# Runs of four U and four V rows instead of eight in the PEER gathers, and another place for the ranking

## The chip, the cores and the metric

The kernel runs on one core of a Trainium2 chip. The metric is the time of one execution in microseconds, measured on the device. Three runs of the kernel before gave 5031.24, 5041.35 and 5054.40 us; the median is 5041.35.

## The reference, cut to what matters

One inference step of a two-layer decoder: 512 prompt tokens and 64 sample tokens (8 sequences of 8), width 1024. Layer 0 mixes tokens with latent attention (the samples against 4096 cached positions each), layer 1 with sliding-window attention. After each of the two stands a PEER channel mixer, which is where this change lies:

```python
q = (xt @ w_q).reshape(n, PEER_HEADS, 2, PEER_HALF)
s = jnp.einsum('nhpd,hpkd->nhpk', q, sub_keys)
s_top, i_top = lax.top_k(s, PEER_TOPK)                 # 16 of 128, twice per head
cand_s = s_top[:, :, 0, :, None] + s_top[:, :, 1, None, :]
best_s, best_pos = lax.top_k(cand_s.reshape(n, 8, 256), PEER_TOPK)
experts = jnp.take_along_axis(cand_i, best_pos, axis=-1)
gates = jax.nn.softmax(best_s, axis=-1)
act = gelu(jnp.einsum('td,thkd->thk', x, u_tab[experts]))
out = jnp.einsum('thk,thkd->td', gates * act, v_tab[experts])
```

Eight heads choose 16 experts each, so every token reads 128 rows of `u_tab` and 128 of `v_tab`, each of 1024 float32 values (4 KB).

## The kernel before, in words

**Tiles and slots.** Tokens lie on the 128 partitions. There are four tiles of prompt tokens and one of the 64 sample tokens, which is put twice on the partitions, so that it needs half as many slots. A *slot* is one expert position for all 128 tokens of a tile: one gather of U (512 KB, 128 rows of 4 KB) and one of V. A layer has `ALL` = 4 x 128 + 64 = 576 slots, so 1152 gathers. The whole is done twice, by `peer_rows` for layer 0 and for layer 1.

**What a slot needs.** POOL issues both gathers as indirect DMAs (`gather`, L1550 to L1554). DVE multiplies the U row with the normed token and sums it (`dot`, L1582 to L1586). When all dots of a group of `RG` slots are there, ACT takes their gelu (`gelu`, L1773) and DVE multiplies by the gates (`coefs`, L1588). ACT makes a diagonal matrix of each slot's coefficient (`diagonal`, L1778) and PE multiplies it with the V row into two PSUM banks (`mix`, L1871). At the end of a tile DVE adds the banks to the residual (`add`, L1643).

**The ring.** Row buffers form a ring of 16 (`RING`). POOL gathers in runs: U of group 0, U of group 1, V of group 0, U of group 2, V of group 1 and so on, with 8 slots a group (L1561 to L1574). `u_th` and `v_th` (L1440, L1441) give a slot's place in that order. Gather n waits until gather n-16 has been used: for U by its dot (`S_uf`), for V by its mix (`S_vf`). POOL is in order, so one unfree buffer holds up all that come after.

**The order on the engines.** Each engine walks through `now` = 0 to 588 in an order written out by hand. At `now` DVE does `dot(now)`; at `now` = 1 modulo `RG` it does `coefs` of the group before; at 11 of a tile `add` of the tile before. ACT does `diagonal(now - 10)`, then, at a multiple of `RG`, `gelu` of the group that has just ended; PE does `mix(now - 12)`.

**Work for the next tile.** In between, DVE finds the experts of the next tile (L1746 to L1756): `rank` (the best 16 of 256 candidates of a head, eight operations) at 16, 24 to 72; `key_numbers` (three operations on 128 x 2048 elements for either half) at 80 and 84; `number` at 88; `gate` at 96. ACT takes `exps` at 92. POOL waits for `number` (`S_ex`) when it starts on a new tile.

**The first of the two layers** also carries the latent attention of the samples (`latent_step`, 4 steps for each of 72 parts, 16 steps to every 21 slots) and then the sample tile's own projections, keys and ranking (`sample_step`). Each latent step goes over PE, ACT and DVE in turn: DVE waits there for PE's scores (L1663), and ACT takes an exp (L1802), for which it has to load another table than for the gelu. In the second layer `latent` is None, so none of this is there.

Of the kernel before, what the change touches and what calls it, by code (L numbers as in the profile page):

```python
# [46 lines left out]
PH, NK, TOPK, HALF = 8, 128, 16, 128  # L47
# [1196 lines left out]
def rank_head(nc, ch, settled, halves, ranks, hd):  # L1244


    def ranked(ins):
        ch.inc(ins)
        wait_apart(ch.eng, ch.done, ch.base + ch.n, settled)
    cand, rest, best, place = ranks["cand"], ranks["rest"], ranks["best"], ranks["place"]  # L1250
    flat = cand[:].rearrange("p i j -> p (i j)")
    ranked(nc.vector.tensor_tensor(cand[:], halves[0].unsqueeze(2).to_broadcast([P, TOPK, TOPK]),
                                   halves[1].unsqueeze(1).to_broadcast([P, TOPK, TOPK]), ALU.add))
    ranked(nc.vector.max(best[:, 0:8], flat))
    ranked(nc.vector.max_index(place[:, 0:8], best[:, 0:8], flat))
    ranked(nc.vector.match_replace(rest[:], best[:, 0:8], flat, -3e38))
    ranked(nc.vector.max(best[:, 8:16], rest[:]))
    ranked(nc.vector.max_index(place[:, 8:16], best[:, 8:16], rest[:]))
    ch.inc(nc.vector.tensor_copy(ranks["all_best"][:, bass.ds(hd * TOPK, TOPK)], best[:]))
    ch.inc(nc.vector.tensor_copy(ranks["all_places"][:, bass.ds(hd * TOPK, TOPK)], place[:]))  # L1260
    wait_apart(ch.eng, ch.done, ch.base + ch.n, settled)
# [150 lines left out]
def peer_rows(nc, a, sbuf, sem, bank, x, ident, mod, junk, stat, layer, h2, best, key, ranks, mod_rows, landed, latent=None):  # L1412
# [1 line left out]

    tag = f"px{layer}_"
    s = ExitStack()
    RG = 8
    RD = 8
    KEEP = 4 * RG
    ALL = NTP * HK + PAIRED  # L1420
    GROUPS = ALL // RG
    PER_TILE = HK // RG
    DIAG_AT, MIX_AT = 10, 12
    ST = NTP * HK - HK
# [14 lines left out]
    bvt, bpt = ranks["all_best"], ranks["all_places"]  # L1439
    u_th = lambda slot: slot if slot < RG else slot // RG * 2 * RG - RG + slot % RG  # L1440
    v_th = lambda slot: (slot // RG + 1) * 2 * RG + slot % RG if slot < ALL - RG else slot + ALL  # L1441
    landings = lambda n: 16 * (layer * (2 * ALL // RING) + n // RING + 1)
# [10 lines left out]
    if latent is not None:  # L1453
# [46 lines left out]
        def latent_steps(now):  # L1500
            return range(-(-16 * now // 21), min(-(-16 * (now + 1) // 21), 4 * (PARTS + 1)))
# [5 lines left out]
    with nc.Block() as block:  # L1507
# [40 lines left out]
        @block.gpsimd  # L1548
        def _(pool):
            def gather(table, slot, n):  # L1550
                if n >= RING:
                    freed, slots = released(n - RING)
                    pool.wait_ge(freed, slots)
                pool.indirect_dma_start(row_buf[n % RING][:], None, table, offset(ap=experts[:, slot:slot + 1], axis=0)).then_inc(landed[n % RING], 16)  # L1554

            def released(n):
                return (S_uf, u_slot[n] + 1) if n in u_slot else (S_vf, v_slot[n] + 1)

            u_slot = {u_th(slot): slot for slot in range(ALL)}
            v_slot = {v_th(slot): slot for slot in range(ALL)}  # L1560
            for g in range(GROUPS + 1):  # L1561
                if g < GROUPS:
                    if g % PER_TILE == 0:
                        pool.wait_ge(S_ex, g // PER_TILE + 1)
                    if latent is not None and g == 53:
                        pool.wait_ge(S_xss, 1)
                        nc.gpsimd.tensor_tensor(sq[:, 1:2], sq[:, 0:1], stat[:, 3:4], ALU.add).then_inc(S_add, 1)
                        pool.wait_ge(S_add, 1)
                        nc.gpsimd.tensor_tensor(sq[:, 1:2], sq[:, 1:2], stat[:, 4:5], ALU.pow).then_inc(S_xr, 1)
                    for slot in range(g * RG, (g + 1) * RG):  # L1570
                        gather(u_tab, slot, u_th(slot))
                if g >= 1:
                    for slot in range((g - 1) * RG, g * RG):
                        gather(v_tab, slot, v_th(slot))  # L1574

        @block.vector
        def _(dve):
# [4 lines left out]
            def dot(slot):  # L1582
                dve.wait_ge(landed[u_th(slot) % RING], landings(u_th(slot)))
                u = row_buf[u_th(slot) % RING]
                nc.vector.scalar_tensor_tensor(out=u[:], in0=u[:], scalar=1.0, in1=h2[:, tile_of(slot), :], op0=ALU.mult, op1=ALU.mult,  # L1585
                                               accum_out=dots[:, slot % KEEP:slot % KEEP + 1]).then_inc(S_uf, 1)  # L1586

            def coefs(g):  # L1588
                t, first = tile_of(g * RG), g * RG % HK
                cols = slice(g * RG % KEEP, g * RG % KEEP + RG)  # L1590
                dve.wait_ge(S_g, g + 1)
                if g >= KEEP // RG:
                    dve.wait_ge(S_d, RG * (g - KEEP // RG + 1))
                for rows, more in HALVES if t == NTP else [(slice(0, P), 0)]:
                    last = nc.vector.tensor_tensor(coef[rows, cols], gelus[rows, cols], e[rows, t, first + more:first + more + RG], ALU.mult)  # L1595
                last.then_inc(S_c, 1)

            def rank(t, hd):
                ch.round(t * PER + hd * HEAD)
                rank_head(nc, ch, (S_in, 32), [bestv[:, t * 2 * PH + hd * 2 + half, :] for half in range(2)], ranks, hd)  # L1600
# [31 lines left out]
            def gate(t):  # L1632

                ev = e[:, t, :].rearrange("p (h k) -> p h k", h=PH)
                dve.wait_ge(S_exp, t + 1)
                nc.vector.tensor_reduce(esum[:, :, 0], ev, AX_X, ALU.add).then_inc(S_gate, 1)
                dve.wait_ge(S_gate, t * 3 + 1)
                nc.vector.reciprocal(esum[:], esum[:]).then_inc(S_gate, 1)
                dve.wait_ge(S_gate, t * 3 + 2)
                nc.vector.tensor_tensor(ev, ev, esum[:].to_broadcast([P, PH, TOPK]), ALU.mult).then_inc(S_gate, 1)  # L1640
                dve.wait_ge(S_gate, t * 3 + 3)

            def add(t, g, rows):  # L1643
                dve.wait_ge(S_vf, min(HK * (t + 1), ALL))
                if t:
                    dve.wait_ge(S_out, 3 * t)
                for n in range(2):
                    nc.vector.tensor_tensor(junk[0:rows, n * 512:(n + 1) * 512], bank[n][0:rows, :],
                                            g[0:rows, n * 512:(n + 1) * 512], ALU.mult).then_inc(S_out, 1)
                dve.wait_ge(S_out, 3 * t + 2)  # L1650
                nc.vector.tensor_tensor(x[0:rows, t, :], x[0:rows, t, :], junk[0:rows, :], ALU.add).then_inc(S_out, 1)
# [84 lines left out]
            for now in range(ALL + MIX_AT + 1):  # L1736
                if now < ALL:
                    dot(now)
                if now == 4:
                    gate(0)  # L1740
                if now % RG == 1 and RG <= now <= ALL + RG:
                    coefs(now // RG - 1)
                t, at = divmod(now, HK)
                if at == MIX_AT - 1 and 1 <= t <= NTP:
                    add(t - 1, mod[0][:, 2 * D:3 * D], P)
                if t + 1 < (NT if latent is None else NTP):  # L1746
                    if 16 <= at < 16 + 8 * PH and at % 8 == 0:
                        rank(t + 1, at // 8 - 2)
                    if at == 80:
                        key_numbers(t + 1, 0)  # L1750
                    if at == 84:
                        key_numbers(t + 1, 1)
                    if at == 88:
                        number(t + 1)
                    if at == 96:
                        gate(t + 1)  # L1756
                if latent is not None:
                    for k in latent_steps(now):
                        latent_step(k)
                    sample_step(now)  # L1760
# [318 lines left out]
```

## Time and profile before

| what | value |
| --- | --- |
| median of three runs | 5041.35 us |
| profiled execution, its own time | 5044.04 us |
| its span | 5041.9 us |
| mean granted TensorE clock | 0.855 |
| gathers of the first PEER layer | 1152, in 852 to 2596 us |
| gathers of the second PEER layer | 1152, in 3384 to 5005 us |
| bytes gathered (queue q0) | 1208.11 MB of 1381.48 MB |
| median time from issue to landing, U and V | 6.8 and 6.6 us |

The page sums one execution over its whole length. The stretches of the two PEER layers are read from windows of the trace, since the other stages have other limits. Durations in a timeline are those of single instructions; in brackets stands the idle time before one and what ended it. "issue" there is a gap in which the engine waited for nothing that the profile shows.

### The profile page before, as it was taken

How to read it: one execution, taken by the hardware profiler on the slowest of the kernel's cores; microseconds unless marked ns; L12 is line 12 of the kernel's file. 1: busy time of each engine (PE TensorE's matmuls, PEld its weight loads, DVE VectorE, ACT ScalarE, POOL GpSimd, SP SyncE). 2: the span in 40 equal slices, each digit the busy share in tenths (PEclk: the TensorE clock that was granted, in tenths of full speed). 3: DMA queues.
4: the chain of work that ended last, by engine and by line, in shares of the span. 5: the costliest groups of instructions: out<-in, count | busy, mean ns of one | idle time of the engine just before them, and what ended most of it. 6: DMA issues, size and time to landing. Idle time of an engine off the chain costs nothing. (4 is left out here: it accounts for less than half of the span.)

```text
span 5041.9 us, 41707 instructions
## 1 busy us (share of the span) xinstructions
PE 3840.2 (76%) x11081; PEld 1863.9 (37%) x11081; DVE 2578.8 (51%) x6419; ACT 975.3 (19%) x2603; POOL 2614.1 (52%) x2407
## 2 busy tenths in 40 slices
PE   2377885999999999677768777856677677676776
PEld 0144543454444444343214543432233233232322
DVE  1115347665665665467421551575545545555543
ACT  0012111334333333111110220111111111111111
POOL 0010001777767777677740000017777877777775
PEclk8689887999999999898879557878888788888888
DMA  9400023999999999999980001229999999999998
GB/s 346 170 6 0 34 64 118 397 372 389 383 356 380 389 365 365 381 371 343 398 308 41 5 15 58 60 69 373 351 394 368 346 394 362 355 393 365 364 394 317
DMA packets 509377, 1381.48 MB, mean 274 GB/s; under 512 B 84466, under 2 KB 176691, under 8 KB 508276
## 3 DMA queue, kind: packets, MB, share of 16 engines
q0 software_dynamic: 331776, 1208.11, 62.8%
q1 hardware_dynamic: 176996, 170.89, 10.6%
q8 instruction: 75, 1.23, 0.1%
q14 instruction: 98, 0.80, 0.0%
q10 hardware_dynamic: 432, 0.44, 0.0%
HBM read 1374.86 MB, written 6.09 MB: 274 GB/s over the span
## 5 line engine op out<-in xcount | busy, mean ns | idle before, releaser
L1585 DVE SCALAR_TENSOR_TENSOR px_rows<-px_rows,h 128x1024 f32<-128x1024 f32 x1152 | 1380.1, 1224 | 992.9 <-DMA px_rows<-in_peer_u,px_experts 978.0
L1880 PE MATMUL bank<-px_rows,px_d 128*128 128x512 f32 (+1 forms) x2304 | 1322.6, 658 | 642.4 <-DMA px_rows<-in_peer_v,px_experts 616.3
L1554 POOL DMA_INDIRECT px_rows<-in_peer_u,px_experts x1152 | 1227.7, 1066 | 784.7 <-DVE px_experts L1629 401.6
L1554 POOL DMA_INDIRECT px_rows<-in_peer_v,px_experts x1152 | 1334.8, 1159 | 415.5 <-issue 309.5
L1881 PE MATMUL bank<-px_rows,px_d 128*128 128x512 f32 (+1 forms) x2304 | 1264.8, 632 | 0.0
L1880 PEld LDWEIGHTS bank<-px_rows,px_d 128*128 128x128 f32 (+1 forms) x2304 | 435.9, 202 | 1210.6 <-issue 1095.2
L1881 PEld LDWEIGHTS bank<-px_rows,px_d 128*128 128x128 f32 (+1 forms) x2304 | 459.8, 200 | 643.6 <-issue 643.6
L1784 ACT ACTIVATE px_d<-ident,px_coef 128x128 f32<-128x128 f32 x1024 | 344.5, 391 | 1107.9 <-DVE px_coef L1595 1085.3
L1386 PE MATMUL bank<-pk_hT,pk_w 128*128 128x512 f32 x512 | 229.9, 603 | 0.0
L1666 DVE TENSOR_REDUCE px_ntop<-bank 128x1 f32<-128x512 f32 (+1 forms) x72 | 46.0, 639 | 322.3 <-PE bank L1903 321.9
L1386 PEld LDWEIGHTS bank<-pk_hT,pk_w 128*128 128x128 f32 x512 | 96.8, 194 | 110.6 <-issue 110.6
L1776 ACT ACTIVATE px_gelus<-px_dots 128x8 f32<-128x8 f32 x144 | 30.0, 208 | 556.2 <-DVE px_rows L1585 555.7
L1013 POOL COPY wt_qs<-qkv 128x1024 f32 x4 | 4.2, 1039 | 242.2 <-POOLq L1056 144.1
L270 PE MATMUL bank<-mr_w,cT 128*9 128x512 f32 x384 | 53.4, 719 | 99.0 <-DMA mr_w<-in_w_mod 99.0
L1912 PE MATMUL bank<-px_room 128*128 128x256 f32 x512 | 121.1, 379 | 0.0
L1304 POOL TENSOR_TENSOR pk_rms_inv<-pk_squares,stat 128x4 f32<-128x4 f32 (+1 forms) x2 | 0.4, 196 | 218.1 <-ACT junk L1315 218.1
L1912 PEld LDWEIGHTS bank<-px_room 128*128 128x128 f32 x512 | 97.2, 190 | 40.8 <-issue 30.9
L993 PE MATMUL bank<-sp_w,sp_hT 128*128 128x512 f32 x240 | 106.6, 604 | 5.9 <-DVE qkv L960 5.1
L1892 PE MATMUL bank<-ident,px_room 128*128 128x128 f32 x512 | 89.6, 277 | 24.0 <-DMA px_room<-in_cache_mla_kpe 24.0
L420 POOL MEMSET rstd<- 128x4 f32 x1 | 0.1, 101 | 194.2 <-POOLq L304 194.2
L682 POOL COPY at_qs<-q 128x384 f32 (+1 forms) x16 | 8.1, 507 | 170.8 <-PE bank L691 170.6
L1585 DVE DVE_READ_ACCUMULATOR px_rows<-px_rows,h 128x1 f32 x1152 | 93.1, 81 | 0.0
(350 smaller groups left out, 4031.9 us busy)
## 6 DMA issues: line engine op xcount, KB each, us to landing
mr_w<-in_w_mod SPq DMA_DIRECT2D x24, 2048.0 KB, 20.1
px_room<-in_cache_mla_ckv SPq DMA_DIRECT2D x256, 128.0 KB, 5.8
px_rows<-in_peer_u,px_experts POOLq DMA_INDIRECT x1152, 6.8
px_rows<-in_peer_v,px_experts POOLq DMA_INDIRECT x1152, 6.6
pk_w<-in_peer_w_q SPq DMA_DIRECT2D x32, 512.0 KB, 3.7
px_room<-in_peer_w_q SPq DMA_DIRECT2D x16, 512.0 KB, 14.2
mod_prompt<-mod_rows SPq DMA_DIRECT2D x4, 1536.0 KB, 6.4
sp_w<-in_swa_w_qkv SPq DMA_DIRECT2D x1, 6144.0 KB, 19.8
```

The source lines that it names most:

```text
L270: last = pe.matmul(bank[STRIPS * (r % 2) + j][strip(j), :], cT[:, c, :], w[r % 2][j][:, c, :], start=(c == 0), stop=(c == DC - 1))
L993: last = pe.matmul(bank[2 + n][:], hT[:, c, :], w[:, c, n * 512:(n + 1) * 512], start=(c == 0), stop=(c == DC - 1))
L1386: last = pe.matmul(wide[:], w[p][:, c, :], hT[:, c, 0:SEQ], start=(c == 0), stop=(c == DC - 1))
L1554: pool.indirect_dma_start(row_buf[n % RING][:], None, table, offset(ap=experts[:, slot:slot + 1], axis=0)).then_inc(landed[n % RING], 16)
L1585: nc.vector.scalar_tensor_tensor(out=u[:], in0=u[:], scalar=1.0, in1=h2[:, tile_of(slot), :], op0=ALU.mult, op1=ALU.mult, accum_out=dots[: ...
L1666: kd.step(nc.vector.tensor_reduce(ntop[:, b % 2, g:g + 1], src, AX_X, ALU.max, negate=True))
L1776: nc.scalar.activation(gelus[:, cols], dots[:, cols], ACT.Gelu).then_inc(S_g, 1)
L1784: nc.scalar.activation(diag[slot % RD][:, 0:shape.shape[1]], shape[:], ACT.Copy, scale=coef[:, slot % KEEP:slot % KEEP + 1]).then_inc(S_d, 1)
L1880: pe.matmul(bank[0][0:m, :], d[:, 0:m], v[:, 0:512], start=first, stop=last)
L1881: pe.matmul(bank[1][0:m, :], d[:, 0:m], v[:, 512:D], start=first, stop=last).then_inc(S_vf, 1)
L1892: pe.transpose(bank[2 + c][:, j * P:(j + 1) * P], page[:, j, c * P:(c + 1) * P], ident[:])
L1912: last = pe.matmul(bank[7][:, 0:KL], probsT[:, j * P:(j + 1) * P], page[:, j, 0:KL], start=(j == 0), stop=(j == GP - 1))
```

## The change

The group size `RG` goes from 8 to 4. So POOL gathers four U rows and four V rows in turn, ACT takes a gelu and DVE the coefficients for four slots at a time; the ring stays at 16 buffers, and `KEEP` (4 x `RG`) becomes 16. The place at which POOL computes the samples' norm in the first layer is written as a slot and stays the same one (424). The steps for the next tile move: `rank` from the first dot of every run of eight (16, 24 to 72) to the last one before it (15, 23 to 71), which ends a run of four; `key_numbers` to 79 and 87; `number` from 88 to 87; `gate` from 96 to 95.

```diff
-    RG = 8
+    RG = 4
     RD = 8
     KEEP = 4 * RG
...
-                    if latent is not None and g == 53:
+                    if latent is not None and g == (ST + 40) // RG:
                         pool.wait_ge(S_xss, 1)
...
                 if t + 1 < (NT if latent is None else NTP):
-                    if 16 <= at < 16 + 8 * PH and at % 8 == 0:
-                        rank(t + 1, at // 8 - 2)
-                    if at == 80:
+                    if 15 <= at < 15 + 8 * PH and at % 8 == 7:
+                        rank(t + 1, at // 8 - 1)
+                    if at == 79:
                         key_numbers(t + 1, 0)
-                    if at == 84:
+                    if at == 87:
                         key_numbers(t + 1, 1)
-                    if at == 88:
                         number(t + 1)
-                    if at == 96:
+                    if at == 95:
                         gate(t + 1)
```

## Rows read from the trace of the kernel before

**Rows 1.** The page, busy us (share of the span) xinstructions.

```profile
PE 3840.2 (76%) x11081; PEld 1863.9 (37%) x11081; DVE 2578.8 (51%) x6419; ACT 975.3 (19%) x2603; POOL 2614.1 (52%) x2407
```

**Rows 2.** Waits of POOL, second PEER layer: total us, times, longest us.

```profile
POOL px_rows L1554 <- issue: 334.6, 1097, 0.3
POOL px_rows L1554 <- PE bank L1881: 12.8, 42, 0.3
```

**Rows 3.** Timeline of DVE beside a ranking: start us, us, instruction.

```profile
3516.38 1.23 DVE L1585 SCALAR_TENSOR_TENSOR px_rows<-px_rows,h 128x1024 f32<-128x1024 f32 x1 [10.13 <-DMA px_rows<-in_peer_u,px_experts]
3517.53 0.42 DVE L1252 TENSOR_TENSOR cand<-best 128x256 f32<-128x256 f32 x1
3520.95 1.23 DVE L1585 SCALAR_TENSOR_TENSOR px_rows<-px_rows,h 128x1024 f32<-128x1024 f32 x1
```

**Rows 4.** Timeline of POOL in the same stretch.

```profile
3505.08 1.97 POOL L1554 DMA_INDIRECT px_rows<-in_peer_v,px_experts  x1 [0.31 <-issue]
...
3509.85 0.93 POOL L1554 DMA_INDIRECT px_rows<-in_peer_u,px_experts  x1 [0.30 <-issue]
3517.30 1.11 POOL L1554 DMA_INDIRECT px_rows<-in_peer_u,px_experts  x1 [0.30 <-issue]
```

**Rows 5.** Stretches, L1585 alone: us, DVE busy (x), PEclk, DMA, GB/s.

```profile
3388.80:4980.80 1592.00, 683.68 (x1136) 0.83 0.98 372
4409.00:4490.90 81.90, 39.47 (x64) 0.81 1.03 409
4830.70:4980.80 150.10, 68.26 (x112) 0.84 1.01 391
```

**Rows 6.** Timelines of DVE and POOL in a stretch without ranking.

```profile
4409.09 1.22 DVE L1585 SCALAR_TENSOR_TENSOR px_rows<-px_rows,h 128x1024 f32<-128x1024 f32 x1 [14.19 <-DMA px_rows<-in_peer_u,px_experts]
...
4429.55 1.23 DVE L1585 SCALAR_TENSOR_TENSOR px_rows<-px_rows,h 128x1024 f32<-128x1024 f32 x1 [10.28 <-DMA px_rows<-in_peer_u,px_experts]
...
4409.65 1.47 POOL L1554 DMA_INDIRECT px_rows<-in_peer_u,px_experts  x1 [0.30 <-issue]
...
4421.62 0.94 POOL L1554 DMA_INDIRECT px_rows<-in_peer_u,px_experts  x1 [0.30 <-issue]
...
4430.31 1.28 POOL L1554 DMA_INDIRECT px_rows<-in_peer_u,px_experts  x1 [0.30 <-issue]
```

**Rows 7.** As rows 5: four stretches with rankings, then four with key numbers.

```profile
3426.40:3608.30 181.90, 75.60 (x128) 0.85 0.98 366
...
sum 735.10, DVE 303.16; mean DVE 75.79
...
sum 293.60, DVE 115.71; mean DVE 28.93
```

**Rows 8.** Stretches: PE, PEld, DVE, ACT, POOL busy, PEclk, DMA; timeline of PE.

```profile
1000.00:2000.00 1000.00, 959.69 (x3038) 486.02 (x3039) 612.16 (x1229) 379.02 (x817) 760.41 (x657) 0.98 1.01 377
3400.00:4900.00 1500.00, 1070.34 (x2110) 448.30 (x2111) 813.01 (x1562) 188.79 (x614) 1176.42 (x1062) 0.83 0.98 371
...
3511.53 1.02 PE L1881 MATMUL bank<-px_rows,px_d 128*128 128x512 f32 x2
...
3513.25 1.02 PE L1881 MATMUL bank<-px_rows,px_d 128*128 128x512 f32 x2
```

**Rows 9.** First PEER layer: waits of POOL and PE, table loads of ACT.

```profile
POOL px_rows L1554 <- PE bank L1881: 90.2, 104, 9.4
...
PE bank L1880 <- DMA px_rows<-in_peer_v,px_experts: 128.1, 33, 9.8
...
L1776 ACT ACT_TABLE_LOAD x48 | 61.6, 1283 | 0.8
L1802 ACT ACT_TABLE_LOAD x45 | 57.7, 1283 | 0.8
```

**Rows 10.** Timelines of DVE and POOL at the key numbers.

```profile
3610.18 2.29 DVE L1612 TENSOR_TENSOR mod_prompt<-px_ijf,px_iota 128x2048 f32<-128x2048 f32 x1
...
3610.65 2.63 POOL L1554 DMA_INDIRECT px_rows<-in_peer_u,px_experts  x1 [0.30 <-issue]
```

## The prediction

> **What bounds the kernel now.** I read the page's list of engines first [rows 1]: no engine is busy all the time, so the share of the whole span says little. The two PEER layers must be read by themselves. The first one has the latent attention of the samples woven in; the second has not. Together they are two thirds of the span (the table above the change has where they stand).
>
> *Second PEER layer.* The waits of POOL in this stretch [rows 2] decide it. POOL waits 334.6 us in 1097 pieces of at most 0.3 us for nothing ("issue", the gap between two gathers), and only 12.8 us for a buffer that PE must free. So no buffer is short: POOL issues its gathers back to back, and its own rate sets the end. An undisturbed gather takes 0.93 to 0.94 us and its gap 0.30, so 1.24 us [rows 4]. Eight slots are 16 gathers, 16 x 1.24 = 19.84 us. The layer needs more: 1592.0 us for 1136 vector records, 568 dots and as many reads of their accumulator, which is 71 runs of eight at 22.42 us [rows 5].
>
> Where the rest goes is seen when POOL's and DVE's rows are laid side by side. In a stretch with a ranking, the first dot of a run stands at 3516.38, the ranking from 3517.53 to 3520.95 (3.42 us), and the dots after it find their rows landed and run without a gap [rows 3]. Beside such a chain a gather takes 1.97 us where it took 0.94 [rows 4], about every second one: it seems to wait for the end of a dot. In a stretch with no ranking, 4409 to 4491 us, the dots come as the rows land; only the first two gathers beside them are longer (1.47; in the next run 1.28), as if POOL had found its place between the dots [rows 6]. The same eight slots then take 4429.55 - 4409.09 = 20.46 us [rows 6], and the four such runs 81.9 us, at 409 GB/s and a DMA share of 1.03 against 366 and 0.98 beside rankings [rows 5, 7]. I take 20.46 us to be about the DMA engines' own limit.
>
> The stretches by kind [rows 5, 7]: the four stretches of eight runs with rankings take 735.1 us, 22.97 a run; the four stretches of three runs with the key numbers 293.6 us, 24.5 a run; the last 56 slots, without either but not in the clean pattern, 150.1 us, 21.44 a run.
>
> *First PEER layer.* PE is busy 959.7 of 1000 us at a granted clock of 0.98 [rows 8], and one slot's matmuls take 1.72 us at that clock [rows 8], to which the latent steps come. DMA share is 1.01, and POOL waits 90.2 us for PE [rows 9]. Here PE, DMA and POOL lie close together, PE foremost.
>
> **The change, part by part.** The profiled execution has 5044.0 us (span 5041.9); the median of three runs is 5041.35, so the forecast is made against 5044.0 and then lowered by 2.7.
>
> *Runs of four.* The ring stays: U of slot s still waits for the dot of s-8, V of s for the mix of s-8, and both are 16 gathers apart as before. Bytes, dots, matmuls and gathers stay too. What is new is that dots start afresh twice in eight slots. A start costs POOL what the first gathers beside it lose: in the clean stretch 1.47 - 0.94 = 0.53 and 1.28 - 0.94 = 0.34; beside a rank stretch's first dot 1.11 - 0.94 = 0.17; at worst a whole 1.97 - 0.94 = 1.03 [rows 4, 6]. I take 0.45, the middle of the two clean ones: they are the nearest. A clean run of eight then takes 20.46 + 0.45 = 20.9 us (20.5 if DMA's limit covers it or the start costs 0.17; 21.5 at 1.03).
>
> *Rankings behind the last dot of a run.* After the last dot of four, four V gathers pass: 4 x 20.46/16 = 5.1 us in which DVE has no dot to do. The ranking's 3.42 us lie in it with 1.7 to spare, and the next dots go on at the pace of the landings. The gathers beside the ranking itself show 1.11 and less, so I add 0.1. A run with a ranking falls from 22.97 to 20.9 + 0.1 = 21.0: 32 runs x 1.97 = 63 us gained.
>
> *Key numbers.* At 79 and at 87 (now with `number`) instead of 80, 84, 88. Each block has three operations of 2.29 us [rows 10] and some small ones, about 7.6 us, 2.5 more than the gap, so the four dots behind it run in a chain. A gather beside such an operation takes up to 2.63 us; with the operations back to back POOL gets one gather for each, 2.29 instead of 1.24, 1.05 lost. Per tile: 6 x 1.05 + 8 chained dots at about 0.3 = 8.9 us over 3 x 20.9, together 71.6 against 73.4 now. Four tiles: 7 us gained. `number` comes one slot earlier; its experts are wanted 40 slots later, so nobody waits for it.
>
> *All other runs* of this layer, 71 - 32 - 12 = 27, pay 0.45 each: 12 us lost (none to 29, by the bounds of the start).
>
> Second layer: 63 + 7 - 12 = 58 us gained. With the start at 1.03 it is 71 x 0.58 = 41 less, 17; with the start hidden 71 x 0.45 = 32 more, 90.
>
> *Coefficients and gelus per four.* 72 more gelus and coefs. In the second layer ACT is busy 189 of 1500 us [rows 8]: nothing. In the first, every gelu that follows a latent exp needs its table: 48 and 45 loads of 1.283 us are there [rows 9]. The exp comes every 5.25 slots and the gelu will come every 4, so up to 72 of each: 51 more, 65 us of ACT. ACT is busy 379 of 1000 us [rows 8], and the load is issued before the wait, so I cost it at nothing; without that cover it would be 65 us.
>
> *A longer hold of every fourth V row.* ACT's order is diagonal(now-10) and then gelu. With runs of four, the diagonal of slot 4g+3 stands behind the gelu of run g+2, so its mix waits for the dot of 4g+11, whose U is issued four gathers (5.1 us) after V of 4g+3. I cost it at nothing: the buffer is wanted only 16 gathers, 20.5 us, after its issue (worked in the rivals).
>
> *First layer.* The gaps of DVE there are waits for PE, and a ranking fills them at either place: nothing for the 24 rankings. DVE's dot of the second half of a run no longer sits behind a mix whose V is issued after it, which is a smoother order. PE waits 128.1 us for V rows [rows 9]; I count a tenth of it, 13 us gained, with bounds of 60 gained and 30 lost.
>
> Sum: 58 + 13 = 71 gained, 5044.0 - 71 = 4973, by the median 4970. Own range 4930 to 5012.
>
> One rule of the Trainium skill speaks against this. The page "SBUF — State Buffer", section "Who interferes with whom", says that a VectorE instruction with two inputs in SBUF shuts GpSimd's SBUF reads out until it has ended, whichever issues first winning. By it the loss hangs on the number of dots, which stays; the rows agree that a gather waits for a dot's end, and disagree as far as the same dots cost much less in the clean stretch. By the rule nothing is gained and the time stays near 5040, by the rows it is 4970; the first rival below works out the former from rows.
>
> **The rivals.**
>
> *The dots cost the same in any order* (no gain). Eight dots a run of eight at (22.42 - 19.84)/8 = 0.32 us each stay 22.42: the clean stretch is a lucky phase that runs of four don't find, or starts at 1.03 eat what the rankings give back. For it: the last 56 slots have no ranking and still take 21.44 a run. Against it: four equal runs of 20.46. Time 5040, range 5016 to 5066.
>
> *The fourth mix holds its buffer too long* (slower). From V's issue to the buffer's release: 5.1 us to the issue of U 4g+11; to its dot 3516.38 - 3509.85 = 6.5 us up to 4429.55 - 4421.62 = 7.9 [rows 3, 4, 6]; the dot 1.2; gelu, diagonal and signals some 1.0; the mix 1.7 at full clock, twice that at 1.2 GHz (granted clock of this layer 0.83). That is 15.5 to 18.6 us of 20.5. It decides from 2 to 5 us more, which the key numbers (2.5) nearly give, and a DMA queue that fills would. If half a microsecond of it fell on POOL in each of 288 runs of four, that is 144 us: 5044 - 71 + 144 = 5117. In the first layer PE itself would stand at every fourth slot. The table loads push the same way.
>
> *The first layer gains as well* (faster than forecast). If half of PE's wait for V goes (64 us) and the starts in the second layer cost 0.17 (71 x 0.28 = 20 more than the 58): 5044 - 64 - 78 = 4902. Against it: PE's 960 of 1000.
>
> **How the numbers follow.** Forecast 0.50, no gain 0.20, slower 0.13, more gain 0.17. A measurement can tell about 0.5% (25 us) from no change. Faster is forecast and more gain: 0.67. Same 0.20, slower 0.13. The range leaves out the slower rival and the lower end of the largest gain: 4895 to 5058.
>
> **What would show each step.** Right: in the profile after, runs of eight slots beside rankings at 21 us and above 400 GB/s; the ranking with idle time of DVE behind it; gathers of 1.97 us only beside key numbers; the second layer's 71 runs in about 1534 us instead of 1592. Wrong start price: many gathers of 1.5 to 2 us at the head of each four. Wrong on the hold: POOL's wait for PE far over 12.8 us in the second layer, and PE waiting for diagonals. Wrong on the first layer: its gathers take longer than in the table, with ACT's table loads ahead of a waiting PE.

## The result: 0.5% faster, and what the profile shows

The changed kernel takes 5021.15 us (median of 7 runs, 5014.61 to 5022.73) against 5042.81 us (7 runs, 5031.24 to 5054.40) for the kernel before: ratio 0.9953, 95% interval 0.994 to 0.9966. The forecast was 4970, with an own range of 4930 to 5012. The profiled execution of after has 5021.67 us and a span of 5019.8. The 22 us are a difference of two large numbers. The times from the first to the last gather issued, each from one profiled execution (the ends that the table ahead of the change has, 2596 and 5005, lie 2 to 3 us behind the last issue):

| | before | after | difference |
| --- | --- | --- | --- |
| first PEER layer | 852.1 to 2593.3: 1741 | 851.2 to 2656.6: 1805 | +64 |
| second PEER layer | 3384.4 to 5003.3: 1619 | 3445.1 to 4979.2: 1534 | -85 |

**The second layer**, in windows as in [rows 5, 7] (L1585 alone: us, DVE busy, records, PEclk, DMA share, GB/s): all 71 runs of eight slots; then the sum over the four stretches with rankings, with the first of them; then the same for the key numbers.

```profile
3449.40:4962.50 1513.10, 697.36 (x1136) 0.89 1.00 393
...
3490.10:3656.80 166.70, 78.77 (x128) 0.92 1.02 406
...
sum 671.30, DVE 315.07; mean DVE 78.77
...
3656.80:3724.70 67.90, 29.26 (x48) 0.87 0.97 368
...
sum 270.60, DVE 117.04; mean DVE 29.26
```

32 runs with a ranking take 671.3 us, 20.98 each, where they took 22.97. Twelve at the key numbers take 270.6, 22.6 each, where they took 24.5. The rest, 27 runs, is 571.2 now and was 563.3. Beside rankings the layer moves 402 to 406 GB/s. In the timeline of after (DVE, then POOL: start us, us, instruction, idle before it) a ranking stands behind the fourth dot:

```profile
3524.61 1.22 DVE L1585 SCALAR_TENSOR_TENSOR px_rows<-px_rows,h 128x1024 f32<-128x1024 f32 x1
3525.76 0.08 DVE L1585 DVE_READ_ACCUMULATOR px_rows<-px_rows,h 128x1 f32 x1
3525.76 0.42 DVE L1252 TENSOR_TENSOR cand<-best 128x256 f32<-128x256 f32 x1
...
3531.07 1.23 DVE L1585 SCALAR_TENSOR_TENSOR px_rows<-px_rows,h 128x1024 f32<-128x1024 f32 x1 [1.93 <-DMA px_rows<-in_peer_u,px_experts]
...
3521.68 1.13 POOL L1554 DMA_INDIRECT px_rows<-in_peer_v,px_experts  x1 [0.30 <-PE bank L1880]
3523.11 0.99 POOL L1554 DMA_INDIRECT px_rows<-in_peer_v,px_experts  x1 [0.30 <-issue]
3524.40 0.97 POOL L1554 DMA_INDIRECT px_rows<-in_peer_u,px_experts  x1 [0.30 <-issue]
...
3531.92 1.19 POOL L1554 DMA_INDIRECT px_rows<-in_peer_v,px_experts  x1 [0.30 <-PE bank L1880]
```

DVE still idles 1.93 us after the ranking, for a row that has not landed. The first gather beside each four dots is longer (1.13, 1.19), the others hardly (0.97 to 0.99); the 1.97 of [rows 4] is gone.

**The first layer.** The longest waits of DVE, ACT and POOL there (total us, times, longest us), before and then after:

```profile
DVE px_ntop L1666 <- PE bank L1903: 321.9, 57, 13.4
DVE px_rows L1585 <- DMA px_rows<-in_peer_u,px_experts: 259.9, 65, 17.0
ACT px_gelus L1776 <- DVE px_rows L1585: 144.1, 24, 25.2
```

```profile
DVE px_ntop L1666 <- PE bank L1902: 2.7, 5, 1.4
DVE px_rows L1585 <- DMA px_rows<-in_peer_u,px_experts: 734.5, 247, 11.7
ACT px_gelus L1775 <- DVE px_rows L1585: 625.1, 83, 24.6
POOL px_rows L1554 <- PE bank L1880: 227.8, 155, 15.7
```

Before, DVE was often early and waited 321.9 us for PE's scores; it waited 259.9 us for U rows too, which the prediction left out ("The gaps of DVE there are waits for PE"). Now it is late: it waits 734.5 us for U rows, and ACT, which must take the gelu before it goes on, waits 625.1 us behind it. POOL's wait for V buffers has gone from 90.2 us [rows 9] to 227.8. How the two hang together is seen in 20 us of the timeline of after (POOL, DVE, ACT):

```profile
1065.33 0.94 POOL L1554 DMA_INDIRECT px_rows<-in_peer_v,px_experts  x1 [0.86 <-PE bank L1880]
1068.78 0.94 POOL L1554 DMA_INDIRECT px_rows<-in_peer_v,px_experts  x1 [2.51 <-PE bank L1880]
1070.02 0.94 POOL L1554 DMA_INDIRECT px_rows<-in_peer_u,px_experts  x1 [0.30 <-issue]
...
1077.55 1.23 DVE L1585 SCALAR_TENSOR_TENSOR px_rows<-px_rows,h 128x1024 f32<-128x1024 f32 x1 [5.91 <-DMA px_rows<-in_peer_u,px_experts]
...
1083.77 0.20 ACT L1775 ACTIVATE px_gelus<-px_dots 128x4 f32<-128x4 f32 x1 [7.63 <-DVE px_rows L1585]
```

The fourth V gather of a run waits 2.51 us for a mix. The U gather behind it in POOL's queue needs no such buffer, but can start only then; its row is there 7.53 us later, where DVE has been idle for 5.91 us, and ACT waits 7.63 us for the dots.

### The profile page after: what moved, and what is told of

The parts are those of the page before. It is cut to its first block and busy times, and to the rows that moved or that the text cites. A ratio compares the mean times of both kernels' runs of the same rounds, so it can differ in the third digit from the quotient of the medians.

```text
span 5019.8 us, 42343 instructions
## 1 busy us (share of the span) xinstructions
PE 3854.4 (77%) x11081; PEld 1850.7 (37%) x11081; DVE 2612.5 (52%) x6579; ACT 1052.9 (21%) x2799; POOL 2488.4 (50%) x2407
## 5 line engine op out<-in xcount | busy, mean ns | idle before, releaser
L1585 DVE SCALAR_TENSOR_TENSOR px_rows<-px_rows,h 128x1024 f32<-128x1024 f32 x1152 | 1403.7, 1225 | 1379.2 <-DMA px_rows<-in_peer_u,px_experts 1361.3
L1554 POOL DMA_INDIRECT px_rows<-in_peer_u,px_experts x1152 | 1186.4, 1030 | 752.0 <-DVE px_experts L1629 401.4
L1554 POOL DMA_INDIRECT px_rows<-in_peer_v,px_experts x1152 | 1249.2, 1084 | 553.2 <-PE bank L1880 287.1
L1879 PEld LDWEIGHTS bank<-px_rows,px_d 128*128 128x128 f32 (+1 forms) x2304 | 425.1, 199 | 1138.4 <-ACT px_d L1783 647.5
L1880 PEld LDWEIGHTS bank<-px_rows,px_d 128*128 128x128 f32 (+1 forms) x2304 | 457.3, 198 | 634.0 <-issue 634.0
L1775 ACT ACTIVATE px_gelus<-px_dots 128x4 f32<-128x4 f32 x288 | 59.1, 205 | 1954.5 <-DVE px_rows L1585 1953.4
L1801 ACT ACTIVATE px_room<-bank,px_bias 128x512 f32<-128x512 f32 (+1 forms) x72 | 46.5, 645 | 283.9 <-DVE px_bias L1667 283.6
L1585 DVE DVE_READ_ACCUMULATOR px_rows<-px_rows,h 128x1 f32 x1152 | 94.8, 82 | 0.0
```

What stands on the lines that cost most here:

```text
L1775: nc.scalar.activation(gelus[:, cols], dots[:, cols], ACT.Gelu).then_inc(S_g, 1)
L1801: nc.scalar.activation(probs[:, 0:cols], bank[5][:, 0:cols], ACT.Exp, bias=bias[:, b % 2, g:g + 1], scale=MLA_SCALE, accum_out=total[:, b ...
L1879: pe.matmul(bank[0][0:m, :], d[:, 0:m], v[:, 0:512], start=first, stop=last)
L1880: pe.matmul(bank[1][0:m, :], d[:, 0:m], v[:, 512:D], start=first, stop=last).then_inc(S_vf, 1)
```

## The experiments

Two questions: what brings the second layer's 85 us, and what costs the first layer's 64. For the second: the ranking's place (chained dots hold up gathers) or the shorter runs. For the first, three theories: **lead** (V's buffers are freed by a mix 12 steps behind, and U is queued behind V), **tables** (ACT's loads between gelu and exp rise from 48 + 45 to 74 + 69, 50 x 1.283 = 64 us, just the loss), and **hold** (the diagonal of slot 4g+3 behind the gelu of run g+2, a rival of the prediction). "Layer 1" and "layer 2" in the table are the first and the second PEER layer, first to last gather in the profiled execution; "before" in its ratio is always run beside it. The medians are of 4 runs, of 7 for before and after, 9 for e5 and 2 for e7. e5, e7 and e12 give other results than the reference; what each leaves out or changes is said there.

| kernel | median us | ratio, 95% | layer 1 | layer 2 |
| --- | --- | --- | --- | --- |
| before | 5042.8 | | 1741 | 1619 |
| after | 5021.2 | 0.9953 (0.9940 to 0.9966) | 1805 | 1534 |
| e1 fours, new places in layer 2 only | 4953.7 | 0.9829 (0.9810 to 0.9848) | 1733 | 1544 |
| e2 eights, new places | 4936.3 | 0.9792 (0.9775 to 0.9809) | 1731 | 1519 |
| e3 fours, old places | 5113.4 | 1.0149 (1.0125 to 1.0172) | 1846 | 1587 |
| e4 after, mix 8 behind | 4899.7 | 0.9720 (0.9702 to 0.9737) | 1709 | 1515 |
| e5 after, one table | 5020.0 | 0.9963 (0.9949 to 0.9978) | 1808 | 1536 |
| e6 after, diagonal 8 behind | 5013.7 | 0.9945 (0.9922 to 0.9967) | 1809 | 1538 |
| e7 before, one input | 4879.6 | 0.9680 (0.9660 to 0.9699) | 1706 | 1476 |
| e8 e2, mix 16 behind | 4951.1 | 0.9827 (0.9811 to 0.9843) | 1758 | 1504 |
| e9 after, mix 7 behind | 4901.7 | 0.9722 (0.9706 to 0.9738) | 1722 | 1511 |
| e10 e2, mix 11 behind | 4950.8 | 0.9826 (0.9810 to 0.9843) | 1746 | 1518 |
| e11 after, mix 10 behind | 4935.9 | 0.9780 (0.9756 to 0.9804) | 1735 | 1529 |
| e12 e4, twos in layer 1 | 4893.6 | 0.9699 (0.9677 to 0.9722) | 1707 | 1512 |

**e1: each layer by itself.**

```diff
-    RG = 4
+    RG = 8 if latent is not None else 4
...
+                if latent is not None and t + 1 < NTP:
+                    if 16 <= at < 16 + 8 * PH and at % 8 == 0:
+                        rank(t + 1, at // 8 - 2)
...
```

> Runs of four and the new places for the ranking in the second PEER layer alone; the first keeps runs of eight and its old places. If the change pays in the second layer and costs in the first, as its profile shows (gathers of the second 1534 us instead of 1619 from first to last, of the first 1805 instead of 1741), this kernel keeps the gain of 85 and loses the cost of 64: about 5043 - 85 = 4958 us. Rival, that both layers are coupled (through the weights' loads or where the queues stand when the second begins): near 5020.

4953.7 us, where 4958 was expected: each layer keeps its own share. In the second layer 75 of the 85 us gained are there (1544), in the first the loss is gone (1733).

**e2: the places without the runs of four.**

```diff
-    RG = 4
+    RG = 8
```

> Runs of eight as before, only ranking, key numbers, number and gate at their new places, in both layers. If the second layer's gain comes from dots that no longer run in a chain behind the ranking, it needs only the places: behind the last dot of eight there are eight V gathers, 10 us, for a ranking of 3.4 and even for the key numbers' 7.6. Then the second layer's gathers take 1530 us or less and the first stays at 1741: about 4955 us in all. Rival, that runs of four bring the gain (fewer dots in a row beside POOL): second layer near 1600, in all near 5030.

4936.3 us, and the second layer is 1519 us: **the places alone bring all of the second layer's gain**, 100 us of it, and 15 more than with runs of four. The first layer doesn't care for the places (1731 against 1741, within what two profiled executions differ; e1 with the old places has 1733). POOL's waits in the first layer are as before:

```profile
POOL px_rows L1554 <- PE bank L1880: 73.9, 86, 7.6
POOL px_rows L1554 <- DVE px_rows L1585: 33.9, 16, 6.0
```

**e3: the runs of four without the places.** The edit against the changed kernel:

```diff
-                    if 15 <= at < 15 + 8 * PH and at % 8 == 7:
-                        rank(t + 1, at // 8 - 1)
+                    if 16 <= at < 16 + 8 * PH and at % 8 == 0:
+                        rank(t + 1, at // 8 - 2)
...
```

> Runs of four in both layers, ranking and key numbers at their old places (16, 24 to 72; 80, 84, 88; 96). By the theory of the chained dots, the ranking now stands behind the first dot of a run of four, so it holds three dots of eight instead of seven: the second layer gains about a third to a half, 1575 to 1595 us, and the first loses as the changed kernel does, 1805: about 5075. Rival, that runs of four alone bring the second layer's gain: 1535 there, 5020 in all.

The second layer is as expected, 1587 us: with the ranking behind the first dot of four, three dots are chained rather than seven, and 32 us of the 85 are there. The first lost 105 us, 41 more than I had expected, so the whole is 5113.4, 1.5% slower than before. In the first layer the old places do cost, once runs are of four; POOL's wait for PE there is 289.8 us, against 227.8 in after. That a ranking ahead of the gelu of a late run makes it later still is a reading, no run separates it.

**e4: the mix four steps earlier.**

```diff
-    DIAG_AT, MIX_AT = 10, 12
+    DIAG_AT, MIX_AT = 6, 8
```

> The changed kernel with the diagonals 6 and the mixes 8 steps behind the dots, instead of 10 and 12. Theory of the order: PE frees the V buffer of slot 4g-5 at its step 4g+7; POOL's gather of V 4g+3 waits for that, and U 4g+8 is queued behind it, though DVE wants it at step 4g+8 and PE's latent steps hang on DVE. Four steps earlier gives the first layer that many slots of lead again: POOL's waits for PE there fall from 226 us to under 100 and its gathers from 1805 to 1740 or less: about 4955 us. Theory of the tables: nothing of this touches the 50 more table loads, so the first layer stays at 1805 and the time at 5020.

4899.7 us, 2.8% faster than before, and the first layer 1709 us, 96 less than in after and 32 less than before. Its waits, to be held against those of after:

```profile
DVE px_rows L1585 <- DMA px_rows<-in_peer_u,px_experts: 418.1, 173, 12.9
DVE px_ntop L1666 <- PE bank L1902: 150.5, 44, 7.7
ACT px_gelus L1775 <- DVE px_rows L1585: 121.1, 53, 8.4
POOL px_rows L1554 <- PE bank L1880: 117.7, 132, 9.0
L1775 ACT ACT_TABLE_LOAD x74 | 94.9, 1283 | 1.3
L1801 ACT ACT_TABLE_LOAD x69 | 88.5, 1283 | 1.2
```

DVE waits for PE again (150.5 us instead of 2.7) and less for U rows (418.1 instead of 734.5); POOL's wait for PE has halved, though not to under 100 as expected. The 143 table loads are all still there.

**e5: no table loads.**

```diff
-                nc.scalar.activation(gelus[:, cols], dots[:, cols], ACT.Gelu).then_inc(S_g, 1)
+                nc.scalar.activation(gelus[:, cols], dots[:, cols], ACT.Gelu if latent is None else ACT.Exp).then_inc(S_g, 1)
```

> The changed kernel with the exp function in the place of the gelu in the first layer, so that its results are not the reference's: it leaves out the table loads between gelu and exp there (143 of 1.283 us). Theory of the tables: the 50 loads that the change added are the 64 us that the first layer lost, so it returns to 1741 or less, 4955 us or less in all. Theory of the order: the loads lie in ACT's waits; a few microseconds to 20 gained, 5000 to 5020.

5020.0 us, first layer 1808, with not one table load left there: nothing. The theory of the tables is out, although its sum fitted the loss to the microsecond.

**e6: the diagonal ahead of the next run's gelu.**

```diff
-    DIAG_AT, MIX_AT = 10, 12
+    DIAG_AT, MIX_AT = 8, 12
```

> The changed kernel with the diagonals 8 steps behind the dots instead of 10; the mixes stay at 12. The diagonal of slot 4g+3 then stands ahead of the gelu of the run 4g+8 to 4g+11, not behind it. If the first layer's loss is the hold of every fourth V row by that gelu, it goes: 1745 us there, 4960 in all, and PE's wait for diagonals in the second layer (394 us) falls too. If it is the mix's place, the first layer gains a little only: 1790 to 1805, 5005 to 5020 in all.

5013.7 us, first layer 1809. The hold by the gelu was real in the second layer: what PE waited for there was the diagonal, and is now the row itself (second layer of after, then of e6):

```profile
PE bank L1879 <- ACT px_d L1783: 393.8, 133, 51.3
```

```profile
PE bank L1879 <- DMA px_rows<-in_peer_v,px_experts: 389.6, 126, 53.4
```

But it cost nothing there and explains nothing of the first layer, where POOL still waits 230.1 us for PE. ACT's wait for the dots in the first layer falls from 625.1 to 214.8 us, and the layer takes as long as before: that wait followed from the late rows and was not the loss.

**e7: dots that read one input.** In the kernel before:

```diff
-                nc.vector.scalar_tensor_tensor(out=u[:], in0=u[:], scalar=1.0, in1=h2[:, tile_of(slot), :], op0=ALU.mult, op1=ALU.mult,
-                                               accum_out=dots[:, slot % KEEP:slot % KEEP + 1]).then_inc(S_uf, 1)
+                nc.vector.tensor_reduce(dots[:, slot % KEEP:slot % KEEP + 1], u[:], AX_X, ALU.add).then_inc(S_uf, 1)
```

> The kernel before, with each dot replaced by a sum over the U row alone, which has one input in SBUF where the dot has two; the product with the token is left out, so the results are not the reference's. The operation is about as long (1.2 us). If a gather waits for the end of a DVE instruction because that reads two SBUF inputs, none is longer than 0.94 us beside these sums, rankings or not: the second layer then runs at the faster of POOL's 19.84 us a run of eight and what the DMA engines allow; at 20.46 everywhere that limit is theirs, at 19.84 it was the dots' too. About 1470 us for its gathers, 4890 in all. If any DVE instruction delays a gather, the second layer stays near 1619 us and the time near 5040.

4879.6 us (two runs) and a second layer of 1476. The timeline is that of a run with a ranking at its old place (DVE, then POOL). Six sums run in a chain as the dots did, and no gather is longer:

```profile
3437.86 1.22 DVE L1585 TENSOR_REDUCE px_dots<-px_rows 128x1 f32<-128x1024 f32 x1
3438.99 0.15 DVE L1594 TENSOR_TENSOR px_coef<-px_gelus,px_e 128x8 f32<-128x8 f32 x1
3439.07 6.84 DVE L1585 TENSOR_REDUCE px_dots<-px_rows 128x1 f32<-128x1024 f32 x6
...
3438.10 0.94 POOL L1554 DMA_INDIRECT px_rows<-in_peer_v,px_experts  x1 [0.30 <-issue]
3439.35 0.94 POOL L1554 DMA_INDIRECT px_rows<-in_peer_v,px_experts  x1 [0.30 <-issue]
3440.59 0.94 POOL L1554 DMA_INDIRECT px_rows<-in_peer_v,px_experts  x1 [0.30 <-issue]
3441.84 0.94 POOL L1554 DMA_INDIRECT px_rows<-in_peer_v,px_experts  x1 [0.31 <-issue]
...
3558.58 2.95 POOL L1554 DMA_INDIRECT px_rows<-in_peer_v,px_experts  x1 [0.30 <-PE bank L1880]
3561.83 2.02 POOL L1554 DMA_INDIRECT px_rows<-in_peer_v,px_experts  x1 [0.30 <-PE bank L1880]
```

The last two stand beside the key numbers, whose products still read two inputs.

The sum differs from the dot in one more thing: it writes one value for each partition where the dot writes back 1024. So e7 by itself doesn't tell the second input from the wide write. The trace of the kernel before does, inside a ranking. Two operations of the same length both write 128 x 256 values; the first reads two wide inputs, the second one (DVE, then POOL):

```profile
3449.04 0.42 DVE L1252 TENSOR_TENSOR cand<-best 128x256 f32<-128x256 f32 x1
3450.56 0.41 DVE L1256 MATCH_REPLACE8 rest<-head_best,cand 128x256 f32<-128x256 f32 x1
...
3449.10 1.17 POOL L1554 DMA_INDIRECT px_rows<-in_peer_u,px_experts  x1 [0.30 <-issue]
3450.57 0.94 POOL L1554 DMA_INDIRECT px_rows<-in_peer_u,px_experts  x1 [0.30 <-issue]
```

The gather that begins in the first is longer, the one in the second is not. Of the gathers of this trace that begin during such an operation, 13 of 14 are over 1 us at the first and none of 14 at the second.

The window over 492 sums, 61.5 runs of eight, shows what is left as the limit:

```profile
3433.20:4700.00 1266.80, 579.17 (x492) 0.88 1.02 407
```

That is 20.6 us a run at 407 GB/s and a DMA share of 1.02. POOL itself is faster here: away from the key numbers it issues 16 gathers in 19.87 us for most of the layer (the four above stand 1.24 us apart), and the rows fall behind. From 3375 to 3550 us the DMA engines move 409 GB/s all the time, and the median time from issue to landing grows from about 7 to about 13 us. Once it is near 13, POOL has to wait for buffers, and eight slots take 20.47 us. So 20.46 is the DMA engines' pace, as I had taken it. (The 85 us that POOL's waits for buffers sum to in this layer are for the most part the ordinary gaps of 0.30; only some 21 us lie above them.)

**e8: runs of eight with as little lead.**

```diff
-    RG = 4
-    DIAG_AT, MIX_AT = 10, 12
+    RG = 8
+    DIAG_AT, MIX_AT = 14, 16
```

> Runs of eight with the ranking at its new places (e2), and the diagonals and mixes four steps later (14 and 16). By the theory of the lead, POOL's gather of U 8G+8 comes behind V 8G-1, which waits for the mix of 8G-9; PE does that at its step 8G+7 instead of 8G+3, one slot ahead of DVE's need, the same as in the changed kernel. So the first layer should lose about what runs of four lost, from 1731 to some 1790 us, with POOL's waits for PE up from 74 us to over 150; about 4995 in all. Rival, that runs of four cost the first layer through more gelus, coefs and turns between U and V: 1731 stays, 4936.

4951.1 us, 15 more than e2; the first layer 1758 instead of 1731, and POOL's wait for PE 161.0 us instead of 73.9. The second layer is 15 us shorter than e2's (1504), which I had not expected and no run explains. DVE's wait for U rows in the first layer, 229.4 us in e2, is here:

```profile
DVE px_rows L1585 <- DMA px_rows<-in_peer_u,px_experts: 574.5, 150, 22.2
```

The direction is that of the lead and the size under half of what I had expected (1790). The head of a run comes here every eight slots instead of every four, which goes the same way.

**e9, e10, e11: a step more or less.**

```diff
-    DIAG_AT, MIX_AT = 10, 12
+    DIAG_AT, MIX_AT = 6, 7      # e9, RG = 4
+    DIAG_AT, MIX_AT = 10, 11    # e10, RG = 8, from e2
+    DIAG_AT, MIX_AT = 8, 10     # e11, RG = 4
```

> Runs of four, diagonals 6 and mixes 7 steps behind the dots (e4 has 6 and 8). If lead is still short in the first layer, a step more of it gains a little more, 1700 us instead of 1709, 4890 in all. If the mix then waits for its diagonal, because ACT makes it only one step before, PE's wait for px_d grows and the first layer loses: 1720, 4910.

> Runs of eight with the ranking at its new places (e2) and the mixes 11 steps behind the dots instead of 12, the least that coefs of eight allow with the diagonals at 10. One slot more of lead in the first layer, where runs of eight have five: 5 to 15 us gained on 4936. It shows whether runs of four are needed at all for the best kernel: with e4 at 4900, they are if this one stays above 4915.

> Runs of four, diagonals 8 and mixes 10 steps behind the dots, between the changed kernel (10 and 12) and e4 (6 and 8). With RG slots in a run and the mix M steps behind, U's lead at the head of a run is RG + 9 - M slots and V's is M + 9 - 2 RG. Here 3 and 11; the changed kernel has 1 and 13 (first layer 1805 us), e4 5 and 9 (1709), before 5 and 5 (1741), e8 1 and 9 (1758), e10 6 and 4 (1746). By the leads the first layer takes between 1725 and 1770 us, and the time lies between 4915 and 4965. If the step from 12 to 8 did something else than give U lead, it need not lie between.

e9 is level with e4 (4901.7 us). Its first layer takes 1722 us and PE's wait for diagonals there grows from 14.9 to 37.7 us, so it is nearer to the second of its two expectations. e10 missed: it lost 14 us on e2 where I expected 5 to 15 gained. With runs of eight, U and V have five slots of lead each, and a step earlier takes from V what it gives to U: POOL's wait for PE stays (65.7 us) and that for dots, which I hadn't counted, doubles:

```profile
POOL px_rows L1554 <- PE bank L1880: 65.7, 79, 8.4
POOL px_rows L1554 <- DVE px_rows L1585: 65.0, 27, 5.3
```

e11 lies between after and e4 as it should: 1735 us between 1805 and 1709.

**e12: runs of two in the first layer.**

```diff
-    RG = 4
+    RG = 2 if latent is not None else 4
...
-    DIAG_AT, MIX_AT = 10, 12
+    DIAG_AT, MIX_AT = (4, 6) if latent is not None else (6, 8)
```

> Runs of two in the first layer, diagonals 4 and mixes 6 steps behind the dots, the second layer as in e4. By the same formulas U's lead is 5 and V's 11 slots, as good as e4's 5 and 9: the first layer should take 1709 us or a little less, 4890 to 4905 in all. Against it stand 72 more... that is, 288 gelus and coefs in place of 144 there, with at most a handful more table loads (an exp comes only every 5.25 slots), and four starts of the dots in eight slots beside POOL: if these cost, 1730 to 1760 and 4920 to 4950.

4893.6 us and a first layer of 1707. It goes on where the lead points, but is level with e4 (the intervals overlap). In this kernel the coefficients of the first two slots come one step ahead of `gate(0)` and so use gates that are not yet divided by their sum; its results are therefore not the reference's, the work is the same.

## Why the prediction was wrong

**The second layer: right in its mechanism, one term too small.** In my own terms, run by run:

| term | forecast | measured |
| --- | --- | --- |
| rankings, 32 runs | 63 gained | 735.1 - 671.3 = 64 gained |
| key numbers, 12 runs | 7 gained | 293.6 - 270.6 = 23 gained |
| other runs, 27 | 12 lost | 571.2 - 563.3 = 8 lost |
| sum | 58 gained | 79 gained (85 from first to last gather) |

A run beside a ranking was put at 21.0 us and is 20.98. The term that was mis-sized is the key numbers', 7 us put and 23 measured: I charged eight chained dots and a fresh start in each of three runs, 71.6 us a tile, and they take 67.65. (The 8.9 us in it need 0.32 for a chained dot; with 0.3 they are 8.7.) I had also let all three operations of a block hold a gather up, 1.05 us each. The trace of after shows that the sum at its end, which reads one input, does not (DVE, then POOL):

```profile
3649.83 2.29 DVE L1612 TENSOR_TENSOR mod_prompt<-px_ijf,px_iota 128x2048 f32<-128x2048 f32 x1
3652.16 2.29 DVE L1613 TENSOR_TENSOR mod_prompt<-mod_prompt,key 128x2048 f32<-128x2048 f32 x1
3654.48 2.29 DVE L1614 TENSOR_REDUCE px_ijf<-mod_prompt 128x128 f32<-128x2048 f32 x1
...
3650.30 2.64 POOL L1554 DMA_INDIRECT px_rows<-in_peer_u,px_experts  x1 [0.30 <-issue]
3653.24 2.02 POOL L1554 DMA_INDIRECT px_rows<-in_peer_u,px_experts  x1 [0.30 <-issue]
3655.57 0.93 POOL L1554 DMA_INDIRECT px_rows<-in_peer_v,px_experts  x1 [0.30 <-issue]
```

Behind each block the chain is only four dots long, and here one gather beside it took 1.97. How the 4 us a tile divide between these and the clean runs, which were put at 20.9, isn't worked out. What the change really uses here is the place: e2 has it with runs of eight. I had charged both parts together and never asked which one carried the gain. In a gap of eight V gathers even the key numbers' 7.6 us fit; by the starts of the gathers, 6 of e2's further 15 us lie in the three runs of each tile around the key numbers (272 us for the twelve, against 278 in after) and another 6 where the tiles change.

The rule of the Trainium skill (page "SBUF — State Buffer", section "Who interferes with whom") that I had set against the change holds, and more exactly than my rows could tell: e7, together with the pair of operations shown there, makes it the second SBUF input of the dot which holds a gather up, for a sum of the same length with one input costs none. What I made of it as a rival was wrong. The dots stayed at 1152 and their price fell: POOL's gathers in the second layer took 1171 us instead of 1269. The rule gives the price of a collision, not how many there are or how late in a dot they fall. In the second layer of before 164 gathers take over 1.5 us, in after 50. Chained dots start 1.15 us apart; at the pace of the landings they start 1.28 us apart, and a gather that then begins just before a dot's end takes 0.97, like the one at 3524.40 above, beside a dot that ends at 3524.55.

**The first layer: the step that failed.** The term is the first layer's 13 us gained, and it rests on this step: "The ring stays: U of slot s still waits for the dot of s-8, V of s for the mix of s-8, and both are 16 gathers apart as before." Every word of it is true, and I drew from it that no gather would start later. POOL's queue is in order, so U of slot 4g+8 also waits for what stands ahead of it: V of 4g+3, hence the mix of 4g-5, which PE does at its step 4g+7. DVE needs U 4g+8 at step 4g+8. In runs of RG slots with the mix M steps behind, the first U of a run has a lead of RG + 9 - M slots and, by the same reckoning for V behind U, the first V has M + 9 - 2 RG:

| | U's lead | V's lead | layer 1 us |
| --- | --- | --- | --- |
| after: 4, 12 | 1 | 13 | 1805 |
| e8: 8, 16 | 1 | 9 | 1758 |
| e11: 4, 10 | 3 | 11 | 1735 |
| before, e2: 8, 12 | 5 | 5 | 1741, 1731 |
| e10: 8, 11 | 6 | 4 | 1746 |
| e4: 4, 8 | 5 | 9 | 1709 |
| e9: 4, 7 | 6 | 8 | 1722 |
| e12: 2, 6 | 5 | 11 | 1707 |

A slot is about 3 us in this layer, and a U row takes 6.5 to 7.9 us from its issue to its dot in the prediction's rows and 7.53 in the 20 us of after shown above, so a lead of one slot isn't enough. Nor does a lead of five take the wait away altogether. Taken from the traces dot by dot, DVE waits for the first U row of a run as follows:

| | first dots that wait | us in all |
| --- | --- | --- |
| after, lead 1 | 132 of 144 | 683 |
| e8, lead 1 | 69 of 72 | 540 |
| e11, lead 3 | 125 of 144 | 560 |
| e4, lead 5 | 100 of 144 | 389 |
| before, lead 5 | 41 of 72 | 238 |
| e2, lead 5 | 28 of 72 | 207 |

In after that is 683 of the 734 us that DVE waits for U rows: the wait sits at the heads of the runs, where the lead puts it. Not all of it is lost, for DVE has idle time anyway. I had asked of the change only whether buffers come free in time, and there I found slack. The second layer has no latent steps that tie PE to DVE; there the same short lead costs little (POOL's waits for PE sum to 59.2 us in 152 pieces instead of 12.8 in 42, but all except some 13 us of it are the ordinary gaps of 0.30; e4 gains 19 us on after). The prediction named "a mix whose V is issued after it" as the bad order of runs of eight and called fours smoother: the sign was the wrong way round for a mix at 12, and right for one at 8, as far as 1709 against 1731 to 1741 can tell.

So the first layer was forecast at 13 us gained, between 60 gained and 30 lost, and lost 64. That loss takes the time out of the forecast's own range. The total misses by 51 us only because the two layers err in opposite directions: the first is 77 us worse than forecast, the second 27 better, which is luck.

**The slower rival** had right symptoms: its two signs, POOL's wait for PE over 12.8 us and PE waiting for diagonals, both stand in the second layer of after (59.2 and 393.8 us), and yet that layer gained 85. They were signs of no cost. e6 took the hold away and gained 7 us in all, within what the intervals allow, and nothing in either layer. Its companion, the table loads, e5 rules out. I had costed the loads at nothing because they are issued before the wait, and that held.

**What stays open.** Within one length of run U's lead orders the kernels (fours: 1805, 1735 and 1709 us at 1, 3 and 5 slots; eights: 1758 and 1731 at 1 and 5), and a sixth slot brings nothing. Across the lengths it doesn't give the size: e8 and after have the same U lead and differ by 47 us. That heads of runs come twice as often in after is my reading: the counts of late first dots, 132 and 69, go with it, but no run shows it alone. Why e3 loses 41 us more than after in the first layer isn't settled either. The profiled spans of a layer scatter by some 10 us (1731 to 1741 for what should be alike), so that 1707, 1709 and 1722 are no order of their own.

## What to carry to other kernels

When a queue in order serves two rings, write down for each gather not only its own buffer's release but that of everything ahead of it, and in which step of which engine that falls; changing the length of the runs moves that lead, and the distance between producer and consumer (here `MIX_AT`) has to move along. With it the same change is worth 2.8% instead of 0.5%. And before a change in two parts is forecast, forecast the parts: the ranking's place alone gave 2.1%.

## What the runs showed of the hardware that I had not expected

- A gather from POOL (0.94 us, then a gap of 0.30) that begins during a DVE instruction with two inputs in SBUF is held until that instruction has ended: 1.97 us beside chained dots, up to 2.95 beside products of 2.29 us. In the traces of before and after it takes about 0.83 us plus what is left of the dot when it begins, and 0.94 where less than some 0.13 us is left (mostly also where it begins in the dot's first 0.05 us). Beside sums as long as the dots (1.22 us) with one input it stays at 0.94, and so it does beside an operation with one wide input that writes 128 x 256 values. With the dots' second input and wide write gone (e7), the second layer is 143 us shorter (1619 to 1476), and then the DMA engines are the limit.
- When dots come at the landings' pace, POOL and DVE fall into step and the loss all but vanishes: 0.97 to 0.99 a gather. The same two engines, with the same work, then run at 402 to 409 GB/s instead of 366.
- With 4 KB rows and 512 KB a gather, 409 GB/s at a DMA share of 1.03 was the most in any window shown here, also where POOL issued faster than that (e7).
